# Layer 1's modulation sums on VectorE, and a written-out conv stage on two sets of PSUM banks

## What is computed

```python
s_lat, s_ctx = silu(c), silu(c_ctx)
for layer in range(2):
    shift, scale, gate = split(s_lat @ ada_w[layer] + ada_b[layer], 3)    # ada_w[layer]: 2048 x 6144
    h = rms_norm(x, pre_g[layer]) * (1 + scale) + shift                   # the same for ctx with s_ctx
    if layer == 0:      # h @ ev_w_in, then per channel group:
        a_out = multiscale_pool(a_v, pool_w, pool_scale, on_grid) * silu(a_g)      # 4 groups
        b_out = b_b * depthwise_conv3(b_c * b_x, conv_w, conv_b) * silu(b_g)       # 8 groups
        y = concatenate([a_out, b_out]) @ ev_w_out
    else:               # h @ od_w_in, 16 heads of a gated chunkwise scan, @ od_w_out
        ...
    x = x + gate * rms_norm(y, post_g[layer])
```

## Time and profile before

| | us |
|---|---|
| three timed executions | 2999.57, 2993.07, 2996.55 |
| their median | 2996.55 |
| span of the profiled execution, first to last instruction | 2985.9 |
| PE busy in it (share) | 2789.8 (93%) |
| DVE busy | 1810.4 (61%) |
| ACT busy | 1343.3 (45%) |
| pool group g = 3 on PE, first matmul to the next group's | 338.26 to 403.95 |
| conv stage on PE, first matmul to the last of its sums | 403.95 to 830.8 |
| `out0`, first matmul | 833.45 |

### The profile page before, as it was taken

How to read it: one execution, slowest core, us unless ns; L and a number is a source line. 1 busy time by engine, 2 the same in 40 slices (tenths; PEclk the granted TensorE clock), 3 DMA queues, 4 the chain that set the end, 5 groups by cost and what they waited for, 6 DMA issues and landing times.

```text
span 2985.9 us, 40704 instructions
## 1 busy us (share of the span) xinstructions
PE 2789.8 (93%) x14145; PEld 2280.2 (76%) x14145; DVE 1810.4 (61%) x2616; ACT 1343.3 (45%) x2019; POOL 0.2 (0%) x4
## 2 busy tenths in 40 slices
PE   5899999999999689999999999987999987999988
PEld 2677777777778578888888888876878766888866
DVE  5966655445452367767677676865656644656654
ACT  5643433333342334444444453545545644545563
POOL 0000000000000000000000000000000000000000
PEclk8999999999999899999999999998999998999999
DMA  8856554455432223323333333344544455544454
GB/s 309 295 185 209 197 180 157 151 161 162 149 125 91 94 85 97 106 88 105 97 89 104 93 100 105 125 155 153 174 156 142 142 182 170 154 159 142 158 167 141
DMA packets 418884, 437.17 MB, mean 146 GB/s; under 512 B 22718, under 2 KB 286536, under 8 KB 417224
## 3 DMA queue, kind: packets, MB, share of 16 engines
q1 hardware_dynamic: 410048, 408.99, 42.9%
q10 hardware_dynamic: 8712, 26.59, 2.5%
HBM read 427.14 MB, written 8.39 MB: 146 GB/s over the span
## 4 chain that ended last, share of the span: by engine, by line
PE 77%; DVE 10%; issue 6%; ACT 4%; DMA 1%; ACTq 1%; DVEq 0%; SPq 0%
PE ps L955 12%; PE ps L956 11%; PE ps L957 11%; PE ps L958 10%; PE ps L960 10%; PE ps L959 10%; DVE wl L1494 3%; PE ps L979 2%; DVE arena L1870 2%; PE ps L981 2%; ACT wh L512 2%; PE ps L1015 1%; DVE arena L1879 1%; PE ps L1195 1%; DMA raw<-in_ada_w_dram 1%
## 5 line engine op out<-in xcount | busy, mean ns | idle before, releaser
L1494 DVE TENSOR_TENSOR wl<-raw,wh 128x1024 fp32r<-128x1024 f32 (+1 forms) x880 | 936.5, 1095 | 701.0 <-ACT wh L512 683.5
L512 ACT ACTIVATE wh<-raw 128x1024 fp32r<-128x1024 f32 (+1 forms) x880 | 807.4, 953 | 881.7 <-PE ps L957 579.9
L955 PE MATMUL ps<-hTh,wh 128*128 128x512 f32 (+1 forms) x2112 | 778.9, 369 | 28.6 <-DVE wl L1494 20.5
L956 PE MATMUL ps<-hTl,wh 128*128 128x512 f32 (+1 forms) x2112 | 764.5, 362 | 0.0
L957 PE MATMUL ps<-hTh,wl 128*128 128x512 f32 (+1 forms) x2112 | 762.8, 361 | 0.0
L958 PE MATMUL ps<-wh,hTh 128*128 128x512 f32 (+1 forms) x1440 | 576.3, 400 | 23.4 <-DVE wl L1494 13.9
L960 PE MATMUL ps<-wh,hTl 128*128 128x512 f32 (+1 forms) x1440 | 558.6, 388 | 0.0
L959 PE MATMUL ps<-wl,hTh 128*128 128x512 f32 (+1 forms) x1440 | 557.5, 387 | 0.0
L955 PEld LDWEIGHTS ps<-hTh,wh 128*128 128x128 f32 x2112 | 399.1, 189 | 108.3 <-DVE wl L1494 38.0
L956 PEld LDWEIGHTS ps<-hTl,wh 128*128 128x128 f32 x2112 | 399.3, 189 | 62.2 <-issue 1.0
L957 PEld LDWEIGHTS ps<-hTh,wl 128*128 128x128 f32 x2112 | 398.5, 189 | 62.6
(11 more groups left out here) (248 smaller groups left out, 2011.2 us busy)
## 6 DMA issues: line engine op xcount, KB each, us to landing
raw<-in_ada_w_dram SPq DMA_DIRECT2D x96, 1024.0 KB, 7.0
raw<-in_w_in_dram SPq DMA_DIRECT2D x88, 1024.0 KB, 5.2
raw<-in_od_w_in_dram SPq DMA_DIRECT2D x256, 320.0 KB, 3.5
raw<-in_ev_w_in_dram SPq DMA_DIRECT2D x192, 256.0 KB, 3.7
raw<-in_w_out_dram SPq DMA_DIRECT2D x32, 1024.0 KB, 5.2
raw<-in_ev_w_out_dram SPq DMA_DIRECT2D x16, 1024.0 KB, 5.1
raw<-in_od_w_out_dram SPq DMA_DIRECT2D x16, 1024.0 KB, 5.1
x_save<-arena ACTq DMA_DIRECT2D x6, 1024.0 KB, 7.6
```

The lines of the kernel that those rows point to most:

```text
L512: nc.scalar.activation(wh[:, ch.spl, part], raw[:, ch.raw, part], ACT.Copy).then_inc(s_hi, 1)
L955: nc.tensor.matmul(out, w_h, x_h, start=first, stop=False, skip_group_check=True)
L956: nc.tensor.matmul(out, w_h, x_l, start=False, stop=False, skip_group_check=True)
L1494: nc.vector.tensor_tensor(wl[:, ch.spl, part], raw[:, ch.raw, part], wh[:, ch.spl, part].bitcast(F32), ALU.subtract).then_inc(s_lo, 1)
```

## The change

Layer 1's 48 modulation chunks leave PE. `ada_row`, `ada_turn`, `hi` and `lo` are not run for them. DVE takes each chunk as it lies in `raw` (now 2 slabs of 1024 columns) and multiplies it with the silu values as per-partition scalars into an accumulator `acc[:, v]`, v the latent or context vector: 4 instructions of 128x1024 a chunk (`ada_products`), 8 chunks a sum of 1024 columns, 6 sums `q`. PE then adds over the 128 partitions (`ada_reduce`: 16 float32 matmuls of one column with `acc` as the weights), and DVE adds the bias (`ada_sum`). The chunks lie in the ring where the table below says; of the two split slots only projection chunks and layer 0's sums take part (`piece` counts those, `half` all).

| stage | modulation chunks before | after |
|---|---|---|
| pool, each of 4 groups | 8 on PE | 4 on PE (layer 0's last 4 blocks) |
| conv, each of 8 groups | 4 on PE | 4 on DVE, after the third and the fourth projection chunk |
| out0 | none | 16 on DVE, between m = 3 and m = 13 |

The conv loop is written out on all engines, and group j uses the banks 4(j % 2) to 4(j % 2) + 3; PE waits for the moves of group j-2 instead of j-1. `ada_reduce` runs behind the first chunk of conv groups 2, 4, 6, behind slab 3 of block 0 and slab 13 of block 1 of `out0`, and before `gate_rows(8)`.

```diff
-POOL_AT = (0, 3, 6, 10)
-POOL_ADA = (1, 2, 4, 5, 7, 8, 9, 11)
+POOL_AT = (0, 2, 4, 6)
+POOL_ADA = (1, 3, 5, 7)
+CONV_AT = (0, 1, 2, 5)
+CONV_ADA = (3, 4, 6, 7)
+OUT_ADA = {3: 2, 4: 2, 5: 2, 6: 2, 8: 1, 9: 1, 10: 2, 11: 2, 12: 1, 13: 1}
...
 # tensor
+            def ada_reduce(q, bank):
+                pe.wait_ge(s_lo, later(q, 7).half(1))
+                for v in range(2):
+                    for t in range(8):
+                        ins = nc.tensor.matmul(psR(bank)[:, t, v:v + 1], acc[:, v, t * P:(t + 1) * P], ones[:, 0:1],
+                                               start=(v == 0 and t == 0), stop=(v == 1 and t == 7), skip_group_check=True)
+                ins.then_inc(s_qP, 1)
...
-                for i in range(12):
+                for i in range(8):
...
-                    if i == 0 and g:
-                        ada_turn(8 + 2 * g)
-                    if i == 5 and g:
+                    if i == 2 and g:
+                        ada_turn(8 + g)
+                    if i == 4 and g:
                         if g > 1:
                             pe.wait_ge(s_py, g - 1)
                         mix(g - 1)
-                    if i == 6:
-                        ada_turn(9 + 2 * g)
...
-            with pe.Fori(1, 8) as j:
-                pe.wait_ge(s_ce, j)
-                pe.wait_ge(s_cx, j)
-                conv_chunk(j, 0)
-                ada_turn(j + 16)
-                for i in range(1, 8):
-                    conv_chunk(j, i)
+            for j in range(8):
+                if j == 1:
+                    pe.wait_ge(s_py, 4)
+                    pe.wait_ge(s_adaT, 13)
+                if j >= 2:
+                    pe.wait_ge(s_ce, j - 1)
+                    pe.wait_ge(s_cx, j - 1)
+                if j in (3, 5, 7):
+                    pe.wait_ge(s_qT, j // 2)
+                for c in range(4):
+                    proj4(st.chunk("conv", j, CONV_AT[c]), c, bank=4 * (j % 2))
+                    if j == 0 and c == 0:
+                        ada_turn(12)
+                    if j == 0 and c == 2:
+                        pe.wait_ge(s_py, 3)
+                        mix(3)
+                    if j in (2, 4, 6) and c == 0:
+                        pe.wait_ge(s_cx, j)
+                        ada_reduce(j // 2 - 1, 5)
...
 # vector
+            def ada_products(q, i):
+                ch = later(q, i)
+                dve.wait_ge(s_raw[ch.raw], ch.arrived)
+                for t in range(2):
+                    for v in range(2):
+                        w = raw[:, ch.raw, t * 2 * BLK:(t + 1) * 2 * BLK]
+                        k = v * KT + 2 * i + t
+                        if i == 0 and t == 0:
+                            ins = nc.vector.tensor_scalar(acc[:, v, :], w, silc[:, k:k + 1], None, ALU.mult)
+                        else:
+                            if t:
+                                dve.wait_ge(s_acc, 16 * q + 2 * i + v + 1)
+                            else:
+                                dve.wait_ge(s_lo, later(q, i - 1).half(v))
+                            ins = nc.vector.scalar_tensor_tensor(out=acc[:, v, :], in0=w, scalar=silc[:, k:k + 1], in1=acc[:, v, :],
+                                                                 op0=ALU.mult, op1=ALU.add)
+                        ins.then_inc(s_lo if t else s_acc, 1)
...
-                for i in range(0 if g else 2, 12):
+                for i in range(0 if g else 2, 8):
                     if i == 0 and g:
                         pool_v(g - 1)
                     lo(st.chunk("pool", g, i))
                     if i == 1 and g:
-                        ada_row(8 + 2 * g, st.chunk("pool", g - 1, 11))
+                        ada_row(8 + g, st.chunk("pool", g - 1, 7))
                         pool_gate(g - 1)
                         pool_rows(g - 1, POOL_WINDOWS[g - 1])
-                    if i == 4 and g:
-                        ada_columns(8 + 2 * g)
+                    if i == 3 and g:
+                        ada_columns(8 + g)
                         pool_means(g - 1, POOL_WINDOWS[g - 1])
...
-                    if i == 10 and g:
+                    if i == 6 and g:
                         pool_out(g - 1)
...
+            pool_v(3)
+            lo(st.chunk("conv", 0, 0))
+            lo(st.chunk("conv", 0, 1))
+            ada_row(12, st.chunk("pool", 3, 7))
+            pool_gate(3)
+            pool_rows(3, POOL_WINDOWS[3])
+            lo(st.chunk("conv", 0, 2))
+            ada_columns(12)
+            pool_means(3, POOL_WINDOWS[3])
+            ada_products(0, 0)
+            ada_products(0, 1)
+            lo(st.chunk("conv", 0, 5))
+            pool_out(3)
+            ada_products(0, 2)
+            ada_products(0, 3)
...
+            for j in range(1, 8):
+                lo(st.chunk("conv", j, 0))
+                conv_x(j - 1)
+                lo(st.chunk("conv", j, 1))
+                conv_mix(j - 1)
+                lo(st.chunk("conv", j, 2))
+                if j in (2, 4, 6):
+                    ada_sum(j // 2 - 1, 5)
+                ada_products(j // 2, 4 * (j % 2))
+                ada_products(j // 2, 4 * (j % 2) + 1)
+                lo(st.chunk("conv", j, 5))
+                ada_products(j // 2, 4 * (j % 2) + 2)
+                ada_products(j // 2, 4 * (j % 2) + 3)
```

More of the change, by code:

```diff
@@ L159, in chunk @@
         upto = 16 * sum(l for j, l in enumerate(loads[:c + 1]) if j % RAW == slot)
-        return Chunk(it * (2 * len(loads)) + 2 * (self.base[name] + c), slot, (self.base[name] + c) % SPL,
+        cuts = len(loads) - len(whole)
+        at = self.cutbase[name] + sum(j not in whole for j in range(c))
+        return Chunk(it * (2 * len(loads)) + 2 * (self.base[name] + c), it * (2 * cuts) + 2 * at, slot, at % SPL,
                      it * per + (self.rawbase[name][slot] + upto))
@@ L356, in first_block_and_hybrid @@
         gp = small[:, 328:360].rearrange("p (k v) -> p k v", v=2)
+        out0 = lambda m: st.chunk("out0", 0, OUT_AT[m])
+        later = lambda q, i: st.chunk("conv", 2 * q + i // 4, CONV_ADA[i % 4]) if q < 4 else st.chunk("out0", 0, OUT_SUM[8 * (q - 4) + i])
         st = Stream([
             ("ada", 8, [1] * 4),
-            ("pool", 4, [4 if i in POOL_AT else 1 for i in range(12)]),
-            ("conv", 8, [4, 1] * 4),
-            ("out0", 2, [1] * 8),
+            ("pool", 4, [4 if i in POOL_AT else 1 for i in range(8)]),
+            ("conv", 8, [4 if i in CONV_AT else 1 for i in range(8)], CONV_ADA),
+            ("out0", 1, [1] * 32, OUT_SUM),
             ("hg", 16, [2] * 8),
@@ L597, in pool_move @@
                     act.wait_ge(s_py, g)
[L598 removed]
+                act.wait_ge(s_used, st.chunk("pool", g, POOL_AT[3]).piece(1))
                 nc.scalar.activation(G2, ps[:, 2:4, :], ACT.Copy)
@@ L642, in high_y @@
                 nc.scalar.activation(hTh[:, k, 0:n], Yk, ACT.Copy).then_inc(s_yh, 1)
-            hi(st.chunk("out0", 0, 0))
+            hi(out0(0))
+            act.wait_ge(s_used, st.chunk("conv", 7, CONV_AT[3]).piece(1))
+            for k in range(4):
+                high_y(k, Y0[:, k, :], TOK)
             conv_move(7)
-            for k in range(8):
+            for k in range(4, 8):
                 high_y(k, Y0[:, k, :], TOK)
-            hi(st.chunk("out0", 0, 1))
+            hi(out0(1))
             act.wait_ge(s_cv, 9)
@@ L1620, in pool_v @@
             def pool_v(g):
-                dve.wait_ge(s_used, st.chunk("pool", g, POOL_AT[3]).half(1))
+                dve.wait_ge(s_used, st.chunk("pool", g, POOL_AT[3]).piece(1))
                 if g:
@@ L1774, in _ @@
                 low_y(k, Y0[:, k, :], TOK, 0)
-            lo(st.chunk("out0", 0, 1))
+            lo(out0(1))
             for k in range(8, KT):
                 low_y(k, Y0[:, k, :], TOK, 0)
-            ada_columns(24)
-            dve.wait_ge(s_adaT, 25)
+            ada_sum(3, 5)
+            dve.wait_ge(s_adaT, 13)
             gate_scale(0)
@@ L1799, in _ @@
                 if m < 16:
-                    lo(st.chunk("out0", m // 8, m % 8))
+                    lo(out0(m))
+                if m == 7:
+                    ada_sum(4, 1)
                 for r in diags.get(m, ()):
@@ L1806, in _ @@
                         dve.wait_ge(s_gbe, 8)
-                    dve.wait_ge(s_used, st.chunk("out0", n // 2, 4 * (n % 2) + 3).half(1))
+                    dve.wait_ge(s_used, out0(4 * n + 3).piece(1))
                     scale_y(4, 4 * (n % 2), n, X4, GB0, 0)
+                for i in range(OUT_ADA.get(m, 0)):
+                    ada_products(4 + summed // 8, summed % 8)
+                    summed += 1
             def residual_add(T, r, arrived, X, buffers):
```

216 lines of the change are left out of this document (109 added, 107 removed).

## The result

The changed kernel takes 2942.4 us (median of 4 runs, 2939.6 to 2945.0) against 2994.8 for the kernel before, timed beside it (4 runs): 0.9821 of its time, 95% interval 0.9807 to 0.9835. The forecast was 2933.5 with a range of 2912 to 2953; so the gain is 52 us where 63 were expected. The profiled execution of the changed kernel took 2939.6 and has a span of 2937.8, at a mean granted clock of 0.966 (0.977 before).

A forecast was written before the change was run, and what follows sets the result against it. PE, busy 93% of the span, was taken as the bound. Against 2996.55 us, -13.1 in pool, -60.0 in conv, +5.2 in out0 and +4.9 before the second head made -63.0: 2933.5 us, range 2912 to 2953.

The forecast's parts named there:

- The bound: Pool and conv: PE bounds, so work leaving it shortens them one for one while DVE keeps ahead; conv group 43.5.
- The start: Whole kernel: 10.65 us lie around the profiled span of 2985.9 and are kept, giving a span near 2923.
- Pool: Pool groups 1 to 3: PE waits 4.0, 5.4, 6.8 for DVE's split before the third projection; stage -13.1 in all.
- the 4.5: Pool: clock loss behind the three PE waits, 1.5 us each, 4.5 in all.
- Conv 0 and 1, DVE's order: Conv: PE waits 2.1 before group 1; later groups have 6.5 of cover, products at 1.20 each.
- The rivals that needed slower products: Conv and out0: products above 1.6 us give 2960, chance 0.12; at 2.4 slower than before, 3093, chance 0.03.
- the one in which the change does nothing: Conv: PE's time is held by something else, such as transfers; about 2997 us, chance 0.03.
- The second set of banks: Conv group starts: nothing waits for the moves any more, 7 x 1.1 = 7.4 us gained.
- The sum over the partitions: Each `ada_reduce` on PE costs 3.9 us with restart, bounds 3.4 and 5.6; three in conv cost 11.7.
- `out0`: Output stage: block 0's sum hidden, -0.5; block 1's costs 3.9; late splits 0.8 and 0.9, together 1.8; +5.2 in all.
- Before the second head: Last sum, before `gate_rows(8)`: 3.9 us plus a 1.0 wait for the first diagonal, +4.9.
- the first rival: Pool without the wait, through a misread order or early columns: gives back 16.1 + 4.5, 2913 us, chance 0.10.

The follow-up runs named there:

- the first experiment: Changed kernel with PE's turn moved early, right behind the first projection chunk of a pool group instead of the third: 2918.3 us, ratio 0.9749.
- the wide sum: Changed kernel with 128 moving columns instead of one in each matmul of the sums: 2929.4 us; with 96 columns and the turn moved early, 2906.3.

## Why the forecast was right, and where it missed

*The bound.* Right. PE's work leaves one for one: a conv group without a sum takes 43.5 as forecast, at clock 1.00 and a DMA share of 0.61 (forecast about 0.6).

*The start.* The 10.65 us that the prediction keeps around the span are not that. An execution takes 1.8 us more than its span (2939.6 and 2937.8; 2996.2 and 2994.4), so the profiled execution of the kernel before was simply a short one, by 9 us. The forecast of the time doesn't hang on it, since it starts from the median; the span that goes with 2933.5 would have been 2932 and not 2923.

*Pool.* Right in its mechanism: waits 3.6, 5.0 and 6.5 for 4.0, 5.4 and 6.8. The loss of clock behind them was put at 1.5 each from a half of 3 us; the steps at the lower clock alone lose 2.2 for two of them and 1.8 for the third (11, 11 and 9 steps of 0.2), and with the first step behind each wait it is 0.4 more. In all the late turn costs 23.2 where 20.6 were put. What hides this in the table is luck: the removed chunks and turns were worth more than forecast, 9.6 for 8.4 in group 0 and 27.0 for 25.3 in groups 1 to 3 (197.0 before, 170.1 with the early turn). The Trainium skill ("TensorE: Matmul & The Clock Gate", section "HAM oscillation") lets waits between groups of matmuls put the array back to half rate, and by that rule the 4.5 stood; the trace agrees, and the first experiment took wait and lower clock away together.

*Conv 0 and 1, DVE's order.* Right: 1.87 for 2.1, slack 6.64 for 6.5, product pace 1.20. The rivals that needed slower products fell by the first row of L1624, and the one in which the change does nothing by PE's time in conv. Not counted were the seven matmuls at the lower clock behind the 1.87, 1.4 us; with the early turn the same wait has none behind it (421.21).

*The second set of banks.* Right for the forecast: no group from 2 on waits at its start.

*The sum over the partitions.* This is the term that was mis-sized. Its matmuls were right: 3.7 forecast, 3.63 measured, and the upper bound of 5.6 fell away, since its row was one at the lower clock. The estimate of 3.4 from the Trainium skill ("TensorE: Matmul & The Clock Gate", section "LDWEIGHTS") was close too. But the forecast priced only the instructions and their restart, 3.9, with the clock as the earlier trace rows shows it for conv, while the clock falls behind a sum though PE never idles. In conv a sum cost 5.5: three are 16.4 for 11.7. All six together cost 25 where the forecast had 20.5 for those that it put on the path. By the Trainium skill (same page, section "HAM oscillation"), which speaks there of waits alone, nothing should have happened here; the measurement decides, and the windows at 500 and 593 show the clock down with PE busy all the time.

*`out0`.* Nearly right for the hidden sum: the first two chunks of block 0 take 29.1 (769.24 to 798.33) for 28.4 before, though they hold a whole sum, since PE's wait for the first diagonal shrank from 2.54 to 0.90; the forecast had 0.5 less there, not 0.7 more. The two late splits cost 0.17 and 0.67 for 0.8 and 0.9. The sum in block 1 cost more than 3.9: its stretch takes 28.4 (846.39 to 874.79) for 21.8 before, 6.6 more, of which 0.84 are the two late splits.

*Before the second head.* Mis-sized, 8.7 for 4.9. The sum takes its 3.6 and PE waits 1.29 behind it for the first diagonal (forecast 1.0). Then both pairs of gate matmuls take 2.08 instead of 1.02 and eight projection matmuls run at the lower clock. The experiments split the 8.7: with the sum moved away the stretch takes 72.8, with one matmul of the 16 left 75.7, with the wide sum 78.4 to 79.9 in three kernels, and with the one-column block 80.3 to 81.6 in four, of which the changed kernel is the slowest. So 2.7 to 2.9 are, roughly, the hand-over from PE to DVE and back with what it does to the gates behind, some 3.5 the rest of the sum, and 1.6 between the means what the one-column form costs over the wide one; the last 0.8 are this execution's own.

*The first stage.* No step of the forecast; it wanders by some 5 us from run to run.

The 11 us that are missing by the medians are thus 6 in conv (4.7 at the three sums, 1.4 behind the wait before group 1) and 6 behind it (1.2 at the sum in block 0, 1.9 at the one in block 1, 3.8 before the second head, less 0.9 at the late splits). In conv and in block 1 it is the lower clock behind sum and wait; before the second head the hand-over has its part. And the first rival's 16 + 4.5 us in pool were there to be had.

## What to carry to other kernels

Before a small operation is put into the middle of a dense stretch of TensorE, look in a trace for what its kind does to the clock of the work behind it: its own duration is not its price. A float32 sum over the partitions with one moving column can be given 96 columns of which one counts, at the same duration and without loss of clock, or be put where the engine waits anyway. When DVE's order ties a split behind a step that waits for PE, the turn on PE wants to stand as early as its data allows: moving it two chunks up was worth 23 to 24 us here, nearly half of what the whole change brought.

## What was unexpected

- The granted clock fell with PE 100% busy: 0.66 and 0.83 in the 10 us from a string of one-column float32 matmuls on, 1.00 with 128 columns in the same place.
- In such a string the columns cost next to nothing up to 128: 32 passes with 128x128 weights take 3.63 us with 1 column, 3.71 with 96 and 3.73 with 128. The 5.44 for 32 passes of 128 columns in the earlier trace rows is from a stretch (124 to 131 us) whose granted clock is 0.76; in the four kernels in which the same instructions find it at 1.00 they take 3.81.
- A one-column float32 matmul between two of 512 columns is not hidden at all, 0.23 us each.
- The same wait of 1.87 us before conv group 1 was followed by seven matmuls at the lower clock in the changed kernel (444.03) and by none with the early turn (421.21); of the six kernels that have this wait, three show it and three don't. And the matmuls at the lower clock behind a sum number from 0 to 13 over the runs. What decides it stays open.
